# A decoder block on one core: recurrence levels between projection units, all low parts on VectorE, heads two by two

## The reference

```python
h = rmsnorm(x, norm1_w)
q_a, k_a, v_a, q_b, f_b, i_b, g_b, gate_a, gate_b = split(h @ w_in)   # 7 x 512, 2 x 1024
y_a = moba_attention(rope(q_a), rope(k_a), v_a)      # 8 heads of 64; one block of 256, so causal
y_b = hgrn2(q_b, f_b, i_b, g_b, lb, hgrn_norm_w)     # 4 heads, key and value 128, chunks of 64
mixed = sigmoid(gate_a) * (y_a @ moba_up) + sigmoid(gate_b) * (y_b @ hgrn_up)
x = x + mixed @ w_out
x = x + moe_ffn(rmsnorm(x, norm2_w), ...)            # 32 experts, top 4, clamped SwiGLU
return rmsnorm(x, final_norm_w)
```

## Time and profile before

| | us |
|---|---|
| median of three runs | 1167.89 (1166.47 to 1168.53) |
| the profiled execution, its own time | 1168.07 |
| its span | 1166.3 |
| TensorE busy | 1072.5 (92%) |
| VectorE busy | 347.7 (30%) |
| ScalarE busy | 212.4 (18%) |
| GpSimd busy | 60.3 (5%) |
| chain that ended last | PE 51%, DMA 42%, POOL 3%, DVE 2% |

### The profile page before, as it was taken

One profiled execution on the slowest core, in us unless ns is written; L12 is line 12 of the kernel. 1 busy time (PEld: TensorE's weight loads), 2 busy tenths in 40 slices (PEclk: granted clock), 3 DMA queues, 4 the chain that ended last, 5 costly groups with the idle time before them and its releaser, 6 DMA issues.

```text
span 1166.3 us, 13583 instructions
## 1 busy us (share of the span) xinstructions
PE 1072.5 (92%) x5569; PEld 521.0 (45%) x5569; DVE 347.7 (30%) x646; ACT 212.4 (18%) x337; POOL 60.3 (5%) x39
## 2 busy tenths in 40 slices
PE   6987999999999999988998899898988899989896
PEld 6866999653443434333333233333333333333332
DVE  4896658443221121302020203020303021302122
ACT  4642556311101101010101010101010101010002
POOL 0392003000000000000000000000000000000000
PEclk9998999999999999999999999999999999999999
DMA  8642656889999999999999999999999999999994
GB/s 281 216 146 73 244 189 222 309 344 430 428 427 428 428 429 427 428 429 430 423 429 429 429 428 427 430 428 428 428 429 428 428 430 426 428 429 428 429 425 197
DMA packets 46387, 439.27 MB, mean 377 GB/s; under 512 B 4804, under 2 KB 7128, under 8 KB 21624
## 3 DMA queue, kind: packets, MB, share of 16 engines
q1 hardware_dynamic: 44560, 436.78, 89.8%
q10 hardware_dynamic: 1768, 1.60, 0.4%
HBM read 437.32 MB, written 1.05 MB: 376 GB/s over the span
## 4 chain that ended last, share of the span: by engine, by line
PE 51%; DMA 42%; POOL 3%; DVE 2%; ACT 1%; issue 1%; SPq 0%; POOLq 0%; DVEq 0%; ACTq 0%
DMA S<-in_w_gate_up_dram 19%; PE PS L1514 18%; DMA S<-in_w_down_dram 11%; PE PS L1562 11%; PE PS L1288 8%; DMA EXTRA<-in_w_down_dram 7%; DMA EXTRA<-in_w_gate_up_dram 4%; PE PS L1496 3%; PE PS L1488 3%; PE PS L1251 1%; PE PS L1549 1%; POOL w_lo L370 1%; PE PS L1304 1%; PE PS L1242 1%; POOL S L495 1%; POOL S L494 1%
## 5 line engine op out<-in xcount | busy, mean ns | idle before, releaser
L1514 PE MATMUL PS<-S,M 128*64 128x512 f32 x1664 | 376.1, 601 | 33.0 <-DMA S<-in_w_gate_up_dram 28.4
L1514 PEld LDWEIGHTS PS<-S,M 128*64 128x64 f32 x1664 | 115.6, 137 | 269.5 <-issue 215.3
L1562 PE MATMUL PS<-S,M 128*64 128x512 f32 x800 | 178.7, 595 | 18.5 <-DMA S<-in_w_down_dram 17.6
L1120 DVE TENSOR_SCALAR M<-PS 128x256 f32<-128x256 f32 x64 | 27.1, 423 | 548.6 <-PE PS L1514 548.6
L706 ACT ACTIVATE M<-M 128x256 f32<-128x256 f32 x64 | 26.7, 417 | 502.2 <-DVE M L1120 502.2
L1562 PEld LDWEIGHTS PS<-S,M 128*64 128x64 f32 x800 | 56.5, 137 | 130.0 <-issue 110.1
L711 ACT COPY M<-PS 64x512 f32<-64x512 f32 x31 | 17.9, 578 | 275.4 <-PE PS L1562 275.4
L1134 DVE COPY M<-PS 128x512 f32<-128x512 f32 x32 | 22.2, 692 | 139.0 <-PE PS L1549 139.0
L1488 PE MATMUL PS<-M,XN 128*128 128x128 f32 x512 | 59.8, 275 | 0.0
L1488 PEld LDWEIGHTS PS<-M,XN 128*128 128x128 f32 x512 | 58.5, 192 | 0.5 <-DVE M L1090 0.2
L1496 PE MATMUL PS<-M,SELT 128*128 128x512 f32 x120 | 55.5, 605 | 0.0
(11 more groups left out here) (250 smaller groups left out, 952.1 us busy)
## 6 DMA issues: line engine op xcount, KB each, us to landing
S<-in_w_gate_up_dram SPq DMA_DIRECT2D x104, 2048.0 KB, 43.6
S<-in_w_down_dram SPq DMA_DIRECT2D x49, 2048.0 KB, 42.8
M<-in_w_gate_up_dram SPq DMA_DIRECT2D x12, 2048.0 KB, 43.6
EXTRA<-in_w_gate_up_dram SPq DMA_DIRECT2D x12, 2048.0 KB, 44.6
S<-in_w_in_dram SPq DMA_DIRECT2D x10, 2048.0 KB, 7.9
EXTRA<-in_w_down_dram SPq DMA_DIRECT2D x7, 2048.0 KB, 43.6
M<-in_w_down_dram SPq DMA_DIRECT2D x7, 2048.0 KB, 42.1
S<-in_w_out_dram SPq DMA_DIRECT2D x2, 2048.0 KB, 8.0
```

What stands on the lines that cost most here:

```text
L1120: v.tensor_scalar(gate[:, c], g2[:, :, 0], LIMIT, None, ALU.min).then_inc(gate_ready, 1)
L1514: ins = mm(gu[half][64 * g:64 * g + 64, :], hTe[:, k, tok], gu_slot[slot][:, kk, c:c + 512], start=(k == 0), stop=(k == KD - 1))
L1562: ins = mm(multi[64 * n:64 * n + 64, :], actT[b][:, k, 64 * kh:64 * kh + 64], dn_slot[slot][:, k, 512 * n:512 * n + 512], start=(kh == 0 a ...
```

## The change

- **Units.** D stands between qa0 and qa1, L6 and X behind qa1, and then each of L5 to L0 between two projection units. L6 and X are drained by ScalarE. o0 and o1 come behind g0 and g1, before Q's transposes; each of Q's and K's pair of transposes is followed by a gate unit.
- **Low parts.** All of them are VectorE's (KA, IB and mu were GpSimd's). QA's stand before QB's second half and before the formula of f.
- **GpSimd** has only its memsets and the rope, in the same order of tiles.
- **VectorE and ScalarE.** The logarithm and the scan come before the silu of q; the normalisation of the first tile comes before the small preparations; ScalarE drains half of the transposed tiles. L6's late half reads `bcum` directly.
- **`AT`** has another layout, so a level is copied by one 128-row instruction instead of two of 64 rows. The recurrent output adds the upper half of each chunk by matmuls with 64 rows of contraction, and TensorE waits for itself (`o_upper`) in between.
- **Heads** are taken two by two, with four `SM` buffers; the two heads' score matmuls alternate.

```diff
-PIECES = [(FB, 1, "dve", ("C", 0), None), (QB, 0, "dve", ("C", 1), None), (QB, 1, "dve", ("C", 0), "f1")] + \
-    [(QA, j, "dve", ("A", j), None) for j in range(2)] + [(KA, j, "pool", ("B", j), None) for j in range(2)] + \
-    [(VA, j, "dve", ("A", j), "qa1") for j in range(2)] + [(IB, j, "pool", ("B", j), "ka1") for j in range(2)] + \
+PIECES = [(FB, 1, "dve", ("C", 0), None), (QB, 0, "dve", ("C", 1), None)] + \
+    [(QA, j, "dve", ("A", j), None) for j in range(2)] + [(QB, 1, "dve", ("C", 0), "f1")] + \
+    [(KA, j, "dve", ("B", j), None) for j in range(2)] + [(VA, j, "dve", ("A", j), "qa1") for j in range(2)] + \
+    [(IB, j, "dve", ("B", j), "ka1") for j in range(2)] + \
...
+    u += [("qa0", "act"), ("D", "dve"), ("qa1", "act"), ("L6", "act"), ("X", "act")]
+    u += [("ka0", "act"), ("L5", "dve"), ("ka1", "act"), ("L4", "dve"), ("va0", "act"), ("L3", "dve"), ("va1", "act")]
+    u += [("L2", "dve"), ("ib0", "act"), ("L1", "dve"), ("ib1", "act"), ("L0", "dve"), ("g0", "act"), ("g1", "act")]
+    u += [("o0", "act"), ("o1", "act"), ("qT0", "act"), ("qT1", "act"), ("ga0", "act"), ("kT0", "act"), ("kT1", "act")]
+    fill = iter(["ga1", "ga2", "ga3", "gb0", "gb1"])
+    u += [(next(fill), "act")]
+    for h in range(0, HEADS, 2):
+        u += [(f"sc{h}", "dve"), (f"sc{h + 1}", "dve")]
+        u += [(f"pT{h - 2}", "act"), (f"pT{h - 1}", "act")] if h else []
+        u += [(next(fill), "act")]
...
-                if units == "qa":
-                    for j in range(2):
-                        form_lo(pool, nc.gpsimd.tensor_tensor, KA, j)
...
-            for what, j in ((IB, 0), (IB, 1), ("mu", 0), ("mu", 1), ("mu", 2), ("mu", 3)):
-                form_lo(pool, nc.gpsimd.tensor_tensor, what, j)
...
             lo(FB, 1)
             lo(QB, 0)
+            for j in range(2):
+                lo(QA, j)
 
             wait_drained(ve, "f1")
...
+            silu(0)
             differences(0)
             differences(1)
+            lo(KA, 0)
+            silu(1)
...
+            lo(KA, 1)
+            cross_differences()
             factors(0)
+            factors(1)
+            differences(2)
+            st.settle()
             cross_factors()
...
+            take_level("D", DIAG)
+            factors(2)
             for j in range(2):
                 lo(VA, j)
...
-                            ins = mm(ps[C * b:C * b + C, C * h:C * h + C], lhs[:, h, P * b:P * b + C],
+                            c = C * (GH * b + h)
+                            ins = mm(ps[0:C, c:c + C], lhs[:, h, P * b:P * b + C],
...
+            def recurrent_out(j):
+                ps = begin(f"o{j}")
+                heads = [(T * a, 2 * j + a, slice(P * (2 * j + a), P * (2 * j + a) + P)) for a in range(2)]
+                for o, h, c in heads:
+                    for b in range(2):
+                        mm(ps[:, o + P * b:o + P * b + P], ib[0:CHUNK, b, c],
+                           AT[0:CHUNK, GH * b + h].rearrange("p f t -> p (f t)"), start=(o == 0 and b == 0), stop=True,
+                           skip_group_check=True)
+                for o, h, c in heads:
+                    ins = mm(ps[:, o + P:o + T], ib[:, 0, c], CT[:, h, :], start=False, stop=True, skip_group_check=True)
+                ins.then_inc(o_upper, 1)
+                pe.wait_ge(o_upper, j + 1)
+                for o, h, c in heads:
+                    for b in range(2):
+                        ins = mm(ps[:, o + P * b + CHUNK:o + P * b + P], ib[CHUNK:P, b, c],
+                                 AT[CHUNK:P, GH * b + h, 0, :], start=False, stop=True, skip_group_check=True)
+                end(ins)
...
+            for h in range(0, HEADS, 2):
+                scores(h)
+                if h:
+                    probs_T(h - 2)
+                    probs_T(h - 1)
+                split_T(*GATES[4 + h // 2])
```

More of the change, by code:

```diff
@@ L656, in _ @@
             st.did(nc.scalar.activation(gbT[:], gbT[:], ACT.Sigmoid), sig_ready)
-            round_hi("hu", 0)
-            se.wait_ge(o_ready, 1)
-            st.did(nc.scalar.copy(o_hi.rearrange("p k t -> p (k t)"), oT), o_hi_ready)
-            for j in range(1, 4):
+            for j in range(4):
                 round_hi("hu", j)
@@ L823, in _, with silu @@
             lo(QB, 1)
-            for j in range(2):
-                lo(QA, j)
-            for j in range(2):
+            def silu(j):
                 ve.wait_ge(sgq_ready, j + 1)
@@ L1313, in _ @@
                 split_T(f"q{j}", QB, j)
-            for tt in range(TT):
-                split(f"qa{tt}", QA, tt)
-            for tt in range(TT):
-                split(f"ka{tt}", KA, tt)
             def level(name):
@@ L1368, in _, with scores @@
                     end(ins)
+            def scores(h):
+                both = begin(f"sc{h}"), bank(f"sc{h + 1}")
+                if AT_UNIT[f"sc{h + 1}"] >= BANKS:
+                    wait_drained(pe, UNITS[AT_UNIT[f"sc{h + 1}"] - BANKS][0])
+                for c, q, k in ((0, 0, 0), (128, 1, 1), (256, 1, 0)):
+                    for f, ps in enumerate(both):
+                        r = slice(64 * f, 64 * f + 64)
+                        ins = mm(ps[:, c:c + P], qT[r, h // 2, P * q:P * q + P], kT[r, h // 2, P * k:P * k + P],
+                                 start=True, stop=True)
+                        if c == 256:
+                            if f:
+                                assert begin(f"sc{h + 1}") is not None
+                            end(ins)
             def probs_T(h):
@@ new lines, in _ @@
+            split("qa0", QA, 0)
+            level("D")
+            split("qa1", QA, 1)
+            level("L6")
+            level("X")
+            split("ka0", KA, 0)
+            level("L5")
+            split("ka1", KA, 1)
+            level("L4")
+            split("va0", VA, 0)
+            level("L3")
+            split("va1", VA, 1)
+            level("L2")
+            split("ib0", IB, 0)
+            level("L1")
+            split("ib1", IB, 1)
+            level("L0")
+            split_T(*GATES[0])
@@ L1392, in _ @@
+            split_T(*GATES[1])
             wait_drained(pe, "ib1")
```

276 lines of the change are left out of this document (133 added, 143 removed).

## The result

| | before | after |
|---|---|---|
| median of the runs, us | 1167.92 (4 runs, 1166.47 to 1168.53) | 1159.51 (4 runs, 1158.66 to 1160.45) |
| profiled execution, its own time and span | 1168.07, 1166.3 | 1159.47, 1157.3 |
| first expert product starts at | 249.59 | 239.50 |
| from there to the end of the span | 916.7 | 917.8 |
| GpSimd busy | 60.3 | 35.1 |

The ratio is 0.993 (95% interval 0.9913 to 0.9947). The change gains 8.4 us by the medians and 8.6 us between the two profiled executions, where 13.0 had been forecast. The first expert product comes 10.1 us earlier, not 13.0, and 1.1 us is lost behind it.

The account below looks back on a forecast made before the run. TensorE's path to the experts was taken to bound the kernel, the weight stream following it. Terms 0.4 - 14.7 + 0.3 + 1.2 + 0.4 - 1.6 + 1.0 = -13.0 us gave 1154.9 us; range 1152.5 to 1161.

Parts of the forecast that it names:

- What bounds it: Expert weights stream at the DMA limit from 260 us; bringing TensorE to the experts earlier moves the end by as much.
- Up to q1, +0.4: Start to q1's end: f0 starts earlier, but q1 waits 1.4 us for QB's low part; ends 39.9 instead of 39.45.
- the two old gaps: TensorE's waits before the change, 2.98 us at a recurrence level and 7.62 us for IB's low part; neither expected to return.
- The scan, 2.2 us: VectorE's scan: 6.73 us before, read as about 4.6 us waiting for GpSimd; 2.2 us with GpSimd idle.
- slow by itself: Rival: scan slow without GpSimd, D and X wait 3.2 us, clock may fall; 1158.1 to 1159.8 us, chance 0.14.
- D, L6, X and the levels, -14.7: From scan to L0: no wait at D, X or levels and no slow clock; stalls and clock, 14.7 us, go.
- +0.3 for L6: L6 on TensorE loses alternating output halves: 0.61 us becomes eight products at about 0.11, +0.3 us.
- +0.4 for the switches: TensorE makes two more switches between plain and split matmuls, 0.2 us each.
- TensorE's own work: TensorE's products: L6 +0.3, recurrent output +1.2, switches +0.4, scores two by two -1.6 us.
- Towards the experts, +1.0: Before the experts: mu's low parts on VectorE ahead of ya's make mu0 wait, 19.0 against TensorE's 18.0 us.
- VectorE stays late: Rival: VectorE, with all low parts and rope beside it, falls behind at the levels; 1157 to 1160 us, chance 0.14.
- Rope and VectorE block each other: Rival: GpSimd's rope and VectorE's two-input instructions block each other; at 1.3 us each about 1176 us, slower, chance 0.04.

Follow-up runs that it names:

- experiment 2: Changed kernel plus 22 unread 256-column products on TensorE ahead of q1's wait for its low part; 1157.39 us, ratio 0.9919.
- experiment 1: Changed kernel with QA's low parts behind QB's second one and the scan, their ScalarE roundings behind the logarithm; 1154.44 us, ratio 0.9887.
- experiment 7: Changed kernel plus one unread two-input GpSimd instruction, the size of a low part, released just before the scan; profiled execution 1164.57 us.
- experiment 3: Kernel before with only the low parts of KA and IB moved from GpSimd to VectorE; 1164.13 us, ratio 0.997.
- (4): Changed kernel with the levels back at their old places, low parts all still on VectorE; 1163.18 us, ratio 0.9962.
- (5): Changed kernel with IB's two low parts back on GpSimd behind the rope; 1163.57 us, ratio 0.9969.
- experiment 10: Experiment 1 plus recurrent output's two TensorE self-waits taken together and only mu's first low part ahead of ya's; 1154.54 us, ratio 0.9887.
- experiment 8: Changed kernel with the two heads' score products one head after the other instead of in turns; 1162.20 us, ratio 0.9956.
- 11: Experiment 1 with mu as in experiment 10, and VectorE's cross products straight behind the first level's factors; 1152.77 us, ratio 0.9887.
- experiment 9: Changed kernel again, word for word; 1159.51 us, ratio 0.9937 to the kernel before.
- experiment 6: Changed kernel with KA's two low parts back on GpSimd, ahead of the rope; 1161.36 us, ratio 0.9951.

## Why the prediction was right or wrong

**What bounds it: right.** The stream follows TensorE: the first expert product moved 10.1 us, and from there to the end it is 916.7 us before, and 916.8 to 917.1 us in the five later profiles without a clock fall in the first expert pair.

**Up to q1, +0.4: this is the term that was mis-sized; it is +3.1.** I had the right wait at the right place, and sized it 1.4 us. Two things were missing. QA's weights land at 25.5, not 24.5 us, and the whole of VectorE's chain moves with them: QB's second low part was there at 36.2, where I had 35.1. And I let the clock fall behind the two old gaps, but not behind my own: that takes 1.4 us (experiment 2). The wait is 2.81 us, for TensorE also came to it 0.3 us earlier than I had reckoned. Putting QA behind the scan returns all of it (experiment 1).

**The scan, 2.2 us: right,** 2.28 us alone and 6.67 with one GpSimd instruction beside it (experiment 7). The rival "slow by itself" is out.

**D, L6, X and the levels, -14.7: right.** No level waits and the granted clock is 1.00 from 60 to 120 us. From the end of q1 to the end of the last level or projection behind it TensorE took 107.85 - 39.45 = 68.4 us before and 97.29 - 42.54 = 54.75 now: -13.65, where my steps for it (-14.7, +0.3 for L6, +0.4 for the switches) make -14.0. One reading of mine was wrong without consequence: the level that waited 2.98 us before was level 2, not level 3. But I gave the whole to "neither gap returns" without saying which part of the change earns it. Low parts alone leave 7 us of waits (experiment 3), the levels' new places are needed too (4), and IB on GpSimd would cost 4.1 us again (5). Not tested alone are `AT`'s new layout, the place of the recurrent output and the new order at the start. The layout is the one with a price: 3.1 us of TensorE (below), for a mask copy that takes VectorE 0.75 us a level instead of 1.51. Whether it pays stays open.

**TensorE's own work: partly wrong, and the errors cancel.** The recurrent output is 5.24 us instead of 2.68 (twelve products at 0.22), +2.6 where I had +1.2: the products of 64 columns take 0.26 us each where nothing stands beside them (four in 113.21 to 114.24), and not 0.11, those of 128 columns on 64 rows 0.27 (1.08 / 4) and the cross products 0.32, not 0.22. The two waits of 0.13 us were sized rightly (experiment 10). L6 is 1.08 us, +0.5 where I had +0.3. The scores are 4 x 0.86 = 3.4 instead of 6.35 us, -2.9 where I had -1.6: the two heads do run beside each other in part (experiment 8). I left that for the range because two heads in a row "cost 1.19 against 2 x 0.86"; the Trainium skill's rule ("TensorE: Matmul & The Clock Gate", Part 3) was the better guide, though a pair takes 0.86 and not the 0.7 us that I had drawn from it.

**Towards the experts, +1.0: right,** 1.05 us at mu0; experiments 10 and 11 take it away with one low part moved.

**The sum.** Against my steps the first expert product is late by 2.7 (q1), 1.4 (recurrent output) and 0.2 (L6), early by 1.3 (scores): 3.0 us, and it came at 239.50 where I had said 236.6, 2.9 later. Behind it 1.1 us went to a clock fall that is not in every execution (experiment 9), and 0.4 us lies outside the span (2.2 us now, 1.8 before). 13.0 - 3.0 - 1.1 - 0.4 = 8.5 us, against 8.6 between the two profiled executions.

**Where the time fell: partly luck.** 1159.51 us lies outside the 1153 to 1157.5 that I had given 0.60. It lies inside the outer range, 1152.5 to 1161, whose high end was there for a slow scan and for a VectorE late at the levels, and neither came.

**The rivals.** For a scan of 6.73 us I had D and X late by 2.1 and 1.1 us; by my own times it is 1.8 (42.7 + 4.5 against 45.4) and then some 0.4 more at X (50.5 + 4.5 against 52.8 + 1.8), so this rival was priced about 1 us too high. VectorE was late, but at q1, for weights that came late, and not at the levels as "VectorE stays late" had it. "Rope and VectorE block each other" costs about what I said against it: products of 0.69 us take 1.23 beside the rope, 0.5 us more and not 1, and two low parts 5.57 us instead of 4.49. The levels' slack takes that.

## What to carry to other kernels

A long two-input instruction on GpSimd was paid for here by whichever two-input instruction of VectorE came next (4.3 to 6.7 us instead of 0.7 to 2.3, experiments 5 to 7). Moving such work to the busy engine can be cheaper although it then does all of it, as KA's and IB's low parts were (1.9 and 4.1 us). After such a move the order on that engine is the new limit: work that hangs on a late transfer must stand behind everything that doesn't. And a forecast wait of TensorE should carry the price of the lower clock behind it.

## What the runs showed of the hardware

- A GpSimd instruction with two SBUF inputs holds VectorE's next two-input instruction until it ends: 2.28 to 6.67 us (scan), 0.68 to 4.32, 1.22 to 5.63. With one input in PSUM it passes at 0.69 us (experiment 6).
- In the recurrent output small float32 products have a price that hardly falls with their width: 0.26 us for 64 columns, 0.27 for 128, on 64 rows. Sixteen products of 64 columns on 128 rows whose output halves alternate take 1.08 us (48.10 to 49.18), 0.07 each; L6's eight without alternation take the same 1.08 us, and took 0.61 with it before.
- The granted clock also falls while TensorE is busy: in experiment 10 it is 0.54 and then 0.50 from 109.6 to 113 us with no idle time before. In seven of thirteen profiles it falls within 30 us of the first expert product, and the span from that product on is then 917.8 to 919.8 us; in the other six it is 916.7 to 917.1. What came just before in the changed kernel:

```profile
254.20 3.69 PE L1622 MATMUL PS<-M 32*128 32x512 f32 x8
257.82 0.59 PE L1647 MATMUL PS<-CST,M 128*128 128x128 f32 x2
258.20 1.06 PE L1599 MATMUL PS<-CST,M 128*128 128x128 f32 x4
259.19 11.59 PE L1564 MATMUL PS<-S,M 128*64 128x512 f32 x48
```

  The four records in the third row take 1.06 us here and 0.60 in the kernel before, and the 48 behind them 11.59 instead of 10.52. The same code shows the fall in one profile and not in the next; why is open. Both profiles of the kernel before and its variant (experiment 3) are without it, and seven of the eleven with the changed order have it, so the change may make it more frequent; two profiles are too few to tell.
- f0's 32 records (16 products of plain float32) take 7.14 or 7.15 us in seven profiles and 8.83 to 9.19 in six, both with a granted clock of 1.00 in the records. This too is open.
